# Layer 0's modulation columns beside attention: product on GpSimd, row sum on ScalarE, four transfer buffers

## The chip, the cores and the metric

One core of one Trainium2 chip. The metric is the device time of one execution in microseconds (us); of the kernel before three runs were timed.

## The reference

A batch of one sequence of 512 tokens of width 1024 goes through two blocks of two layers each. The first block is conditioned: its layers start from six modulation vectors, which are one matrix product with the activated condition.

```python
c_act = jax.nn.silu(c)
for l in range(DEPTH):
    mod = c_act @ w_mod[l] + b_mod[l]
    sh_m, sc_m, g_m, sh_f, sc_f, g_f = jnp.split(mod, 6, axis=-1)
    h = rms_norm(x, mix_norm_pre[l]) * (1.0 + sc_m[:, None, :]) + sh_m[:, None, :]
    y = hybrid_mixer(h, positions, w_in[l], ...)
    x = x + g_m[:, None, :] * rms_norm(y, mix_norm_post[l])
    h = rms_norm(x, ffn_norm_pre[l]) * (1.0 + sc_f[:, None, :]) + sh_f[:, None, :]
    y = swiglu(h, w_gate_up[l], w_down[l])
    x = x + g_f[:, None, :] * rms_norm(y, ffn_norm_post[l])
```

Here `c` is one row of 1024 numbers and `w_mod[l]` is 1024 x 6144. The hybrid mixer projects `h`, runs attention with 8 heads of 64 over keys chosen by an index score, runs an mLSTM with 4 heads of 128 beside it, and multiplies the joined heads with `w_out`. The second block has another mixer and no condition. Everything is float32.

## The kernel before, in words

**Modulation columns.** The kernel keeps features on the 128 partitions. The 6144 modulation numbers of a layer are 48 columns of 128. For each column the host has laid out its weights as a tile of 128x1024 (512 KB): row p holds the 1024 weights of feature p. With the activated condition spread over all partitions (`cc`, 128x1024), a column is the product of both tiles, summed along the row. The two layers of the first block have 96 such columns. Columns 0 to 15 (shift and scale of layer 0's mixer) are made before anything else; columns 16 to 39 (`MOD_FIRST` to `MOD_MIX`, 24 of them) beside layer 0's attention; the rest beside layer 0's feed-forward. The change touches the 24 only.

**The streamed weights.** All other weights pass through a ring of four slots of 128x1024. SP loads a slot (L160), ScalarE rounds it to `wh` (L171), GpSimd subtracts to get the rest `wl` (L182, in halves of 512 columns), and TensorE multiplies in three passes (L199 to L201). Each engine has one instruction queue that it takes in order; a wait at its head holds everything behind it.

**The first mixer** (`first_mixer`, used for layers 0 and 1) first runs 30 weight tiles (projections, index scores, the ranking of keys on VectorE, the mLSTM with its products L1022). Then follows attention, without weights from the ring: 32 items (4 blocks of 128 queries from the longest key range down, 8 heads), two in each step. It is written as a loop over steps p = 0 to 19 on each engine, with fixed lags:

- TensorE (L1058 scores of items 2p and 2p+1; L1069 turns the weights of step p-2; L1081 multiplies the weights of step p-3 with the values). In steps 3 to 6 it also turns one mLSTM head (L1090).
- VectorE: the masked row maximum of each score (L1412), one of two copies of turned weights from PSUM to SBUF (L1420, even items); in step 1 it scales the mLSTM results (L1450, four times), in steps 3 to 6 it gates one head (L1457, then L1461 after ScalarE's L1249), and at steps 7, 11, 15 and 19 it sums the squares of a finished block of queries (L1425).
- ScalarE: the copy for odd items (L1235), the exponentials with their row sums (L1227), the gate's rounding (L1249), and at steps 7, 11, 15 and 19 two readings of a finished block (L1244, L1245).

TensorE's turn of a step needs both copies of the step before; a copy needs the values of the same step to have released its buffer.

The 24 columns are spread over steps 2 to 19 on VectorE by `mods_at`, two in steps 4, 7, 10, 13, 16 and 19 and one in the others, at the end of a step (`modulate`, L1303: `tensor_tensor_reduce`, product and row sum in one instruction and a small read of the sum). SP's transfers for them (L877) stand behind its wait for the last mLSTM product (`mout`), and with two buffers, `mod_raw`, each waits for the product two before it:

```python
for n in range(MODS):
    if n == 0:
        sp.wait_ge(mout, MH)
    if n >= 2:
        sp.wait_ge(mod_used, n - 1)
    sp.dma_start(mod_raw[n % 2][:], a["wmod"][48 * rest_of + MOD_FIRST + n]).then_inc(mod_in[n % 2], 16)
```

SP goes on to the ring's loads for the out product after that. GpSimd has no work in attention: its next instruction is an L182 of the out product. The out product's first tiles were prepared before attention.

After step 19 VectorE waits for all 24 columns, adds the bias (L1469), finishes the squares (L1472, L1473); ScalarE, which has loaded the table for roots (L1265) by then, takes the root (L1267); VectorE inverts it (L1475) and scales the attention result (L1478, four times); TensorE turns it (L1110), and ScalarE (L1270) and VectorE (L1482) split it for the second half of the out product. TensorE takes the first half of the first two tiles of the out product, which needs only the mLSTM heads, before L1110.

Layer 1 runs the same code with `rest_of` at None: no columns, no `modulate`.

## Time and profile before

| what | us |
|---|---|
| median of 3 runs | 3232.46 |
| lowest and highest run | 3230.28, 3236.09 |
| the profiled execution's own time | 3230.66 |
| its span, first to last instruction | 3228.9 |
| TensorE busy in the span | 3098.0 (96%) |
| VectorE busy | 1626.8 (50%) |
| ScalarE busy | 1235.4 (38%) |
| GpSimd busy | 1367.8 (42%) |

The profile is of one execution. Its span is the time from the first to the last instruction; the own time has the start and end of the program around it. PE is TensorE's matmul, PEld its weight load, DVE is VectorE, ACT ScalarE, POOL GpSimd, SP SyncE with its DMA queue. Times in the timeline count from the span's start. Names of lines (L1303) are those of the kernel before. PEclk is TensorE's granted clock as a share of 2.4 GHz. "x24 | 29.3, 1224 | 12.3" reads: 24 instructions, 29.3 us busy, 1224 ns each in the mean, 12.3 us of idle time before them.

### The profile page before, as it was taken

Reading aid. Unit: us, or ns where it says so; the run is one execution under the profiler, and the core shown is the slowest. Engines: PE = TensorE matmul, PEld = TensorE weight load, DVE = VectorE, ACT = ScalarE, POOL = GpSimd, SP = SyncE. Lnnn points to the kernel's source line nnn. Section 1 sums busy time; section 2 is a strip of 40 time slices with the busy share of each in tenths; the row PEclk is TensorE's granted clock in tenths of the full one; section 3 lists DMA queues with packets and bytes.
Section 4 is the critical chain, followed back from the end, with each engine's and each line's share of the span. In section 5 each row is a group of like instructions: output and inputs, shape, how many; then the busy total and the mean of one; then the engine's idle time right before and its main releaser. Section 6 shows DMA issues by size and latency. Waiting matters only on the chain.

```text
span 3228.9 us, 39940 instructions
## 1 busy us (share of the span) xinstructions
PE 3098.0 (96%) x14974; PEld 2494.8 (77%) x14974; DVE 1626.8 (50%) x2738; ACT 1235.4 (38%) x2437; POOL 1367.8 (42%) x1167
## 2 busy tenths in 40 slices
PE   6998899999999999999999999999999999999998
PEld 5676778887766788887878788888887777788886
DVE  7787556623686553224344646554244345565521
ACT  3445332233345432232353534443325434343432
POOL 2340255544431254444432544444454234444443
PEclk9999799999999999999999999999999999999999
DMA  5422346622421132222321122222232111222222
GB/s 215 126 79 98 118 167 243 239 97 75 128 72 33 40 101 97 92 95 88 114 86 40 46 78 80 94 96 96 97 112 95 58 42 53 89 80 97 98 91 73
DMA packets 92976, 316.54 MB, mean 98 GB/s; under 512 B 12016, under 2 KB 12656, under 8 KB 92656
## 3 DMA queue, kind: packets, MB, share of 16 engines
q1 hardware_dynamic: 92784, 313.99, 29.1%
q8 instruction: 119, 1.95, 0.2%
q14 instruction: 73, 0.60, 0.1%
HBM read 301.36 MB, written 2.10 MB: 94 GB/s over the span
## 4 chain that ended last, share of the span: by engine, by line
PE 92%; DVE 4%; issue 2%; DMA 1%; ACT 1%; POOL 0%; SPq 0%; DVEq 0%; ACTq 0%; POOLq 0%
PE bank L199 24%; PE bank L201 24%; PE bank L200 24%; PE bank L1842 3%; PE bank L1800 2%; PE bank L1821 2%; PE bank L494 1%; PE bank L919 1%; PE bank L937 1%; PE bank L939 1%; PE bank L938 1%; PE bank L1081 1%; DMA mod_raw<-in_wmod 1%; PE bank L1905 1%; PE bank L1906 1%
## 5 line engine op out<-in xcount | busy, mean ns | idle before, releaser
L182 POOL TENSOR_TENSOR wl<-raw,wh 128x512 fp32r<-128x512 f32 (+1 forms) x952 | 1246.2, 1313 | 1692.8 <-ACT wh L171 1690.6
L171 ACT ACTIVATE wh<-raw 128x512 fp32r<-128x512 f32 (+1 forms) x952 | 587.3, 623 | 1437.3 <-PE bank L201 1340.5
L199 PE MATMUL bank<-hh,wh 128*128 128x512 f32 x2496 | 1005.7, 403 | 36.9 <-DVE hl L553 24.2
L201 PE MATMUL bank<-hh,wl 128*128 128x512 f32 x2496 | 983.5, 394 | 0.0
L200 PE MATMUL bank<-hl,wh 128*128 128x512 f32 x2496 | 983.3, 394 | 0.0
L199 PEld LDWEIGHTS bank<-hh,wh 128*128 128x128 f32 x2496 | 476.0, 191 | 164.0 <-DVE hl L553 30.6
L201 PEld LDWEIGHTS bank<-hh,wl 128*128 128x128 f32 x2496 | 475.3, 190 | 102.8
L200 PEld LDWEIGHTS bank<-hl,wh 128*128 128x128 f32 x2496 | 476.4, 191 | 95.7 <-issue 0.5
L201 PE MATMUL bank<-hidh,wl 128*128 128x512 f32 x704 | 280.8, 399 | 0.0
L200 PE MATMUL bank<-hidl,wh 128*128 128x512 f32 x704 | 277.4, 394 | 0.0
L199 PE MATMUL bank<-hidh,wh 128*128 128x512 f32 x704 | 276.0, 392 | 0.0
L381 DVE TENSOR_TENSOR bank<-x,y 128x512 f32<-128x512 f32 x49 | 63.1, 1289 | 318.7 <-ACT y L360 318.5
L200 PEld LDWEIGHTS bank<-hidl,wh 128*128 128x128 f32 x704 | 132.2, 188 | 34.4
L199 PEld LDWEIGHTS bank<-hidh,wh 128*128 128x128 f32 x704 | 132.2, 188 | 31.4
L201 PEld LDWEIGHTS bank<-hidh,wl 128*128 128x128 f32 x704 | 132.2, 188 | 30.5
L701 DVE SCALAR_TENSOR_TENSOR up<-bank,pc,up 128x511 f32<-128x511 f32 x88 | 65.9, 749 | 160.3 <-ACT up L681 158.8
L743 DVE CAST hidh<-hidden 128x512 fp32r<-128x512 f32 x88 | 123.2, 1400 | 3.0
L741 DVE TENSOR_TENSOR hidden<-gate,bank 128x512 f32<-128x512 f32 x44 | 30.0, 683 | 166.5 <-PE bank L201 158.1
L1968 ACT ACTIVATE tmp<-bank 128x128 f32<-128x128 f32 (+3 forms) x128 | 55.1, 438 | 138.6 <-PE bank L1842 137.1
L701 DVE SCALAR_TENSOR_TENSOR gate<-bank,pc,gate 128x511 f32<-128x511 f32 x88 | 65.9, 749 | 49.7 <-ACT gate L681 48.1
L2077 DVE CUSTOM_DVE_ANT_0 pr<-bank,cst 128x384 f32<-128x384 f32 (+3 forms) x84 | 38.2, 492 | 98.7 <-PE bank L1800 98.6
L490 POOL TENSOR_TENSOR x<-x,y 128x512 f32<-128x512 f32 x49 | 61.9, 1281 | 52.1 <-DVE y L541 52.1
(389 smaller groups left out, 3959.9 us busy)
## 6 DMA issues: line engine op xcount, KB each, us to landing
raw<-in_w SPq DMA_DIRECT2D x444, 512.0 KB, 3.4
mod_raw2a<-in_wmod SPq DMA_DIRECT2D x28, 512.0 KB, 4.5
mod_raw2b<-in_wmod SPq DMA_DIRECT2D x28, 512.0 KB, 5.0
mod_raw<-in_wmod SPq DMA_DIRECT2D x24, 512.0 KB, 3.6
raw<-in_w SPq DMA_DIRECT2D x32, 384.0 KB, 3.0
first_mods<-in_wmod SPq DMA_DIRECT2D x16, 512.0 KB, 13.8
tmp<-rawb SPq DMA_DIRECT2D x72, 64.0 KB, 2.4
turn<-sine SPq DMA_DIRECT2D x56, 64.0 KB, 2.0
```

The costliest lines, as they stand in the source:

```text
L171: act.activation(self.m.wh[:, t % 2, w_], self.m.raw[:, t % RING, w_], ACT.Copy)\
L182: pool.tensor_tensor(self.m.wl[:, t % 2, w_], self.m.raw[:, t % RING, w_], self.m.wh[:, t % 2, w_].bitcast(F32), ALU.subtract)\
L199: pe.matmul(out, wh, xh, start=start, stop=False)
L200: pe.matmul(out, wh, xl, start=False, stop=False)
L201: return pe.matmul(out, wl, xh, start=False, stop=stop)
L381: dve.tensor_tensor(dst, m.x[:, nb, :], m.y[:, nb, :], ALU.mult).then_inc(cross_ready, 1)
L490: pool.tensor_tensor(m.x[:, k, :], m.x[:, k, :], m.y[:, k, :], ALU.add).then_inc(x_ready, 1)
L701: return dve.scalar_tensor_tensor(buf[:, pair, shift:T], bank[:, 0:T - shift], m.pc[:, col:col + 1], buf[:, pair, shift:T], ALU.mult, ALU.add)
L743: step(dve.tensor_copy(hidh[:, q, :], hs[:, pair, :]))
L1800: pe.matmul(ps[one][:, 0:w_], q_, k_, start=True, stop=True).then_inc(score, 1)
L1821: ins = pe.transpose(ps[2 + one][:, kb * P:(kb + 1) * P], prs[i % 6][:, kb * P:(kb + 1) * P], ident)
L1842: ins = pe.matmul(bank[:, h * HD:(h + 1) * HD], m.tmp[:, one, kb * P:(kb + 1) * P], v_, start=(kb == 0), stop=(kb == tb))
```

## The change

The multiply moves to GpSimd: at the end of its work for the mixer's 30 tiles it runs through the 24 columns, waits for each transfer, and multiplies in place. ScalarE sums: at the end of each step, by the same `mods_at`, it waits for the product and runs a Copy over the 128x1024 tile with an accumulated row output into `m.mod`. VectorE no longer takes part; it still waits for `mod_used` after step 19. The two more buffers lie in the second half of `y`'s space, over the tail of `wt` and over `arg` of the mLSTM, which the last mLSTM product ends the use of. The transfer of column n now waits for the sum of column n - 4.

```diff
--- before.py
+++ after.py
@@ -785,7 +785,8 @@
     sc = [m.sq[:, 0, :], m.sq[:, 1, :], rawb[:, 0, :], rawb[:, 1, :]]
 
     cbc = Arena(nc, mix0 + 68 * 1024, D * 4)("cbc", [P, D])
-    mod_raw = [Arena(nc, vm_at + 4 * D * i, 4 * D)(f"mod_raw1{i}", [P, D]) for i in range(2)]
+    mod_raw = [Arena(nc, at, 4 * D)(f"mod_raw1{i}", [P, D])
+               for i, at in enumerate((vm_at, vm_at + 4 * D, y_at + 8 * D, y_at + 12 * D))]
     ang1 = Arena(nc, sel_at, T * 4)("ang1", [P, T])
     posi1 = nc.alloc_sbuf_tensor_at("posi1", [P, T], I32, offset=sel_at)
     turns1, rest1 = rawb[:, 0, :], rawb[:, 1, :]
@@ -797,7 +798,7 @@
     M1_SEMS = tuple(f"bank_free{b}" for b in range(8)) + (
         "latent_sq", "latent_sum", "latent_root", "latent_ready", "sine_ready", "swapped_in0", "swapped_in1", "swapped_in2", "rope_done",
         "conv_base", "conv_done", "ones_set", "order", "act_order",
-        "c_in", "c_act", "mod_in0", "mod_in1", "mod_used",
+        "c_in", "c_act", "mod_in0", "mod_in1", "mod_in2", "mod_in3", "mod_mult", "mod_used",
         "gate_log", "gate_sums", "m_exp", "wi_turned", "wi_ready", "rows_turned", "cols_ready",
         "iscore", "irelu", "irelu_used", "peak_row", "mscore", "arg_ready", "decay", "weight_ready", "masked",
         "mout", "mout_copied", "msums", "mroot_in", "mroot", "mscaled", "mturned", "gated_ready", "mhead",
@@ -812,13 +813,13 @@
         bank_free = sems[0:8]
         (latent_sq, latent_sum, latent_root, latent_ready, sine_ready, swapped_in0, swapped_in1, swapped_in2, rope_done,
          conv_base, conv_done, ones_set, order, act_order,
-         c_in, c_act, mod_in0, mod_in1, mod_used,
+         c_in, c_act, mod_in0, mod_in1, mod_in2, mod_in3, mod_mult, mod_used,
          gate_log, gate_sums, m_exp, wi_turned, wi_ready, rows_turned, cols_ready,
          iscore, irelu, irelu_used, peak_row, mscore, arg_ready, decay, weight_ready, masked,
          mout, mout_copied, msums, mroot_in, mroot, mscaled, mturned, gated_ready, mhead,
          early_ready, score, soft_in, weights, turned, copied_even, copied_odd, pv, out_copied,
          summed, root_in, root, ascaled, aturned, ahead, late_ready) = sems[8:]
-        mod_in, swapped_in = (mod_in0, mod_in1), (swapped_in0, swapped_in1, swapped_in2)
+        mod_in, swapped_in = (mod_in0, mod_in1, mod_in2, mod_in3), (swapped_in0, swapped_in1, swapped_in2)
         sines = rawb[:, 0, :], rawb[:, 1, :], qk[:, 6, :]
         turns_ = m.tmp[:, 0, :], m.tmp[:, 1, :], qk[:, 7, :]
 
@@ -872,9 +873,9 @@
             for n in range(MODS):
                 if n == 0:
                     sp.wait_ge(mout, MH)
-                if n >= 2:
-                    sp.wait_ge(mod_used, n - 1)
-                sp.dma_start(mod_raw[n % 2][:], a["wmod"][48 * rest_of + MOD_FIRST + n]).then_inc(mod_in[n % 2], 16)
+                if n >= 4:
+                    sp.wait_ge(mod_used, n - 3)
+                sp.dma_start(mod_raw[n % 4][:], a["wmod"][48 * rest_of + MOD_FIRST + n]).then_inc(mod_in[n % 4], 16)
 
         def gpsimd(pool):
             s.rests(pool, t0 + 2, t0 + 3)
@@ -888,6 +889,11 @@
                         pool.affine_select(out=w_, in_=w_, compare_op=ALU.is_ge, fill=0.0, base=0,
                                            pattern=[[1, P]], channel_multiplier=-1).then_inc(masked, 1)
                 s.rests(pool, t0 + t + 2, t0 + t + 3)
+            for n in range(MODS):
+                if n == 0:
+                    pool.wait_ge(c_act, 1)
+                pool.wait_ge(mod_in[n % 4], 16 * (n // 4 + 1))
+                pool.tensor_tensor(mod_raw[n % 4][:], mod_raw[n % 4][:], cc[:], ALU.mult).then_inc(mod_mult, 1)
 
         def tensor(pe):
             uses = [0] * 8
@@ -1249,6 +1255,12 @@
                 act.activation(m.hh[:, 4 + h, :], gated[:, h % 2, :], ACT.Identity,
                                scale=pa[:, A_MN + h:A_MN + h + 1]).then_inc(mhead, 1)
 
+            def collect(n):
+                at = 48 * rest_of + MOD_FIRST + n
+                act.wait_ge(mod_mult, n + 1)
+                act.activation(mod_raw[n % 4][:], mod_raw[n % 4][:], ACT.Copy,
+                               accum_out=m.mod[:, at:at + 1]).then_inc(mod_used, 1)
+
             for p in range(STEPS + 1):
                 if p >= VALUE_LAG + 4 and (p - VALUE_LAG) % 4 == 0:
                     finish((p - VALUE_LAG) // 4 - 1)
@@ -1262,6 +1274,8 @@
                     soften(2 * p + 1)
                 if MEND <= p < MEND + MH:
                     gate(p - MEND)
+                for n in mods_at.get(p, ()):
+                    collect(n)
             act.activation(idle4, m.eps[:, 0:1].to_broadcast([P, 4]), ACT.Sqrt)
             act.wait_ge(root_in, 1)
             act.activation(asum, asum, ACT.Sqrt, scale=1.0 / HD).then_inc(root, 1)
@@ -1294,14 +1308,6 @@
                 dve.wait_ge(swapped_in[r % 3], 64 * (r // 3 + 1))
                 dve.tensor_tensor(dst, dst, turns_[r % 3], ALU.add).then_inc(rope_done, 1)
                 dve.wait_ge(rope_done, r + 1)
-
-            def modulate(n):
-                if n == 0:
-                    dve.wait_ge(c_act, 1)
-                dve.wait_ge(mod_in[n % 2], 16 * (n // 2 + 1))
-                raw_, at = mod_raw[n % 2][:], 48 * rest_of + MOD_FIRST + n
-                dve.tensor_tensor_reduce(raw_, raw_, cc[:], 1.0, 0.0, ALU.mult, ALU.add,
-                                         m.mod[:, at:at + 1]).then_inc(mod_used, 1)
 
             freed = [1, 1, 1, 0, 1, 0, 0, 0]
             first_round = {t: sum(rounds_at.get(u, 0) for u in range(t)) for t in range(IN1 + 1)}
@@ -1461,8 +1467,6 @@
                     early(dve.scalar_tensor_tensor(m.hl[:, 4 + h, :], gated[:, h % 2, :],
                                                    pa[:, A_MN + h:A_MN + h + 1], m.hh[:, 4 + h, :].bitcast(F32),
                                                    ALU.mult, ALU.subtract))
-                for n in mods_at.get(p, ()):
-                    modulate(n)
             if MODS:
                 dve.wait_ge(mod_used, MODS)
                 rest = slice(48 * rest_of + MOD_FIRST, 48 * rest_of + MOD_MIX)
```

## Rows read from the trace of the kernel before

**Rows 1.** The page, part 1: busy time, share of the span, instructions.

```profile
PE 3098.0 (96%) x14974; PEld 2494.8 (77%) x14974; DVE 1626.8 (50%) x2738; ACT 1235.4 (38%) x2437; POOL 1367.8 (42%) x1167
```

**Rows 2.** Stretches: span, busy PE, PEld, DVE, ACT, POOL; clock; DMA share; GB/s.

```profile
276.95:353.43 76.48, 56.75 (x320) 48.28 (x320) 54.87 (x132) 30.35 (x83) 0.00 (x0) 0.75 0.50 165
1021.26:1073.83 52.57, 45.83 (x302) 38.88 (x303) 26.60 (x83) 28.77 (x82) 0.00 (x0) 0.86 0.00 1
```

**Rows 3.** The chain that ended last, 276.9 to 353.7, shares by line.

```profile
by line: DMA mod_raw<-in_wmod 29.7%; issue 14.4%; PE bank L1081 11.1%; PE bank L1069 10.0%; DVE mod_raw L1303 10.0%; DVE rawb L1412 4.7%; ACT pr L1227 3.7%; PE bank L1058 3.0%; DVE small L1425 2.3%; PE bank L1090 2.2%; DVE hl L1461 2.0%; AC
```

**Rows 4.** Groups of instructions of VectorE, 262 to 375.

```profile
L1303 DVE CUSTOM_DVE_ANT_0 mod_raw<-mod_raw,cc 128x1024 f32<-128x1024 f32 x24 | 29.3, 1224 | 12.3 <-DMA mod_raw<-in_wmod 11.7
```

**Rows 5.** The tile `mod_raw`, 266 to 269: its first two transfers.

```profile
L877 SPq DMA_DIRECT2D mod_raw<-in_wmod x2: 328/380/433, 267.1 to 267.5; - x2
...
DMA to landing us min/median/max: 3.6/4.1/4.5
```

**Rows 6.** Timeline of GpSimd up to 366; the bracket is idle time before.

```profile
365.10 1.30 POOL L182 TENSOR_TENSOR wl<-raw,wh 128x512 fp32r<-128x512 f32 x1 [101.42 <-ACT wh L171]
```

**Rows 7.** Groups of GpSimd's instructions by form, whole span.

```profile
L490 POOL TENSOR_TENSOR x<-x,y 128x512 f32<-128x512 f32 x49 | 61.9, 1281 | 52.1 <-DVE y L541 52.1
L182 POOL TENSOR_TENSOR wl<-raw,wh 128x256 fp32r<-128x256 f32 x32 | 23.6, 739 | 37.1 <-ACT wh L171 37.1
```

**Rows 8.** The line L182: duration min/median/max in ns.

```profile
L182 POOL TENSOR_TENSOR wl<-raw,wh x952: 738/1295/2357, 8.5 to 3201.4; 128x512 fp32r<-128x512 f32 x184, 128x256 fp32r<-128x256 f32 x7
```

**Rows 9.** Groups of ScalarE's instructions by form, whole span.

```profile
L1186 ACT ACTIVATE cc<-cc 128x1024 f32<-128x1024 f32 x1 | 1.1, 1062 | 0.0
```

**Rows 10.** Timeline of GpSimd at 1932.

```profile
1931.90 2.96 POOL L182 TENSOR_TENSOR wl<-raw,wh 128x512 fp32r<-128x512 f32 x2 [5.19 <-ACT wh L171]
```

**Rows 11.** Timeline of VectorE at 1932.

```profile
1931.99 1.75 DVE L2291 TENSOR_TENSOR y<-y,tmp 128x512 f32<-128x512 f32 x1
1933.77 1.64 DVE L2281 SCALAR_TENSOR_TENSOR hl<-y,hh 128x512 fp32r<-128x512 f32 x1
```

**Rows 12.** The line L541: duration min/median/max in ns.

```profile
L541 DVE TENSOR_TENSOR y<-y,bank x56: 671/676/689, 406.8 to 2850.9; 128x512 f32<-128x512 f32 x56
```

**Rows 13.** The lines L1450 and L1461, both layers.

```profile
L1450 DVE TENSOR_TENSOR num<-num,small x8: 691/692/693, 272.5 to 1019.0; 128x512 f32<-128x512 f32 x8
...
L1461 DVE SCALAR_TENSOR_TENSOR hl<-gated,pa,hh x8: 750/751/752, 284.6 to 1041.2; 128x512 fp32r<-128x512 f32 x8
```

**Rows 14.** ScalarE's waits, 1021.2 to 1041: us in total, times, longest.

```profile
ACT tmp L1235 <- PE bank L1081: 8.5, 4, 3.5
```

**Rows 15.** Timeline of TensorE in layer 0's attention.

```profile
296.52 3.51 PE L1081 MATMUL bank<-va,tmp 128*128 128x64 f32 x16
...
306.36 0.85 PE L1069 MATMUL bank<-cst,pr 128*128 128x128 f32 x6 [0.84 <-ACT pr L1227]
307.05 1.45 PE L1081 MATMUL bank<-va,tmp 128*128 128x64 f32 x12
```

**Rows 16.** Timeline of ScalarE in layer 0, then in layer 1.

```profile
302.32 0.58 ACT L1244 ACTIVATE att_n<-bank 128x512 f32<-128x512 f32 x1
...
353.65 0.23 ACT L1267 ACTIVATE small<-small 128x32 f32<-128x32 f32 x1 [8.17 <-DVE small L1473]
...
1040.98 0.58 ACT L1244 ACTIVATE att_n<-bank 128x512 f32<-128x512 f32 x1
...
1045.07 0.19 ACT L1227 ACTIVATION_READ_ACCUMULATOR pr<-rawb,small 128x1 f32 x1
...
1072.86 1.28 ACT L1265 ACT_TABLE_LOAD   x1
...
1074.27 0.21 ACT L1267 ACTIVATE small<-small 128x32 f32<-128x32 f32 x1
```

**Rows 17.** Stretches of layer 0, columns as in rows 2.

```profile
295.00:303.00 8.00, 8.00 (x37) 6.75 (x35) 5.05 (x11) 3.99 (x11) 0.00 (x0) 0.50 0.36 112
...
322.00:346.00 24.00, 17.89 (x78) 15.70 (x77) 15.40 (x42) 9.27 (x30) 0.00 (x0) 0.52 0.61 196
```


## The prediction

> **What bounds the kernel now.** The page comes first: TensorE is 96% busy [rows 1], so only stretches in which it waits or runs thin can be won. The stage in question is layer 0's attention, and the trace holds a measure for it: layer 1 runs the same code without modulation columns. Set side by side [rows 2], from the same point (TensorE's turn of step 3, after an equal wait, 276.95 and 1021.26) to the same small instruction (L1473, which starts at 353.43 and 1073.83), layer 0 takes 76.5 us and layer 1 52.6. The columns cost 23.9 us today. That is the ceiling of any gain, 0.74% of the span. VectorE is busy 54.9 us in the first stretch and 26.6 in the second, ScalarE about 30 in both.
>
> The chain of waits says how the 23.9 come about: 29.7% of it lies on the landing of a column, 10.0% on VectorE's product [rows 3]. There are 24 products of 1.22 us, and VectorE stands idle 11.7 us for their transfers [rows 4]: with two buffers, a transfer of 3.6 us or more [rows 5] starts only when a product has ended. GpSimd does nothing for 101.42 us up to 365.10 [rows 6].
>
> **The change, part by part.** It takes the 24 products and the 11.7 us of waits out of VectorE's order, has GpSimd multiply and ScalarE sum, and adds two buffers. The transfers stay on SP's queue behind the same first wait; the ring's weight loads queue behind them as before, and the out product starts from ring slots filled earlier, so this costs nothing while the last column is issued no later than now, as it is in the working below.
>
> *GpSimd's product, M.* No GpSimd instruction over 1,024 columns is in the trace. L182 takes 0.739 us for 256 [rows 7] and 1.295 for 512 [rows 8]: 256 columns add 0.556, so 1,024 take 1.295 + 2 x 0.556 = 2.41, an estimate. I take 2.4. Bounds: 2.3, and 2.9 (L182 reaches 2.36 at 512, 1.06 over its median; half of that on each product). 24 products are 57.6 us on an idle engine: room enough in 76 us, not in 52.
>
> *ScalarE's sum.* The Silu over 128x1024 took 1.06 us [rows 9], and the read of a row sum takes 0.19 (L1227 in [rows 16]), part of which I take to lie under the next instruction. I take 1.15, bounds 1.06 and 1.25. 24 are 27.6 us on ScalarE, what VectorE loses. ScalarE waits for GpSimd before each sum, and behind it in its order stand the copies of turned weights that TensorE waits for.
>
> *The shared port.* This is the term against the change. At 1931.9 GpSimd ran two L182 back to back in 2.96 us instead of 2.6 [rows 10]; beside them VectorE's L2291 and L2281, with two SBUF operands each, took 1.75 and 1.64 us [rows 11] instead of the 0.69 of such an instruction alone. They took turns: the second VectorE instruction did not follow the first but waited 0.95, one GpSimd instruction less 0.35. A VectorE instruction with one operand in PSUM does not stretch (L541, 56 times, 0.671 to 0.689) [rows 12]. So the maxima and copies of attention, which read PSUM, are free of it. Two places aren't: L1450, four times in a row from 272.5, and L1461, once in each of steps 3 to 6 [rows 13]. No row shows either beside a busy GpSimd.
> L1450: the first column lands at 267.1 + 3.6 = 270.7 [rows 5]; GpSimd holds the port to about 272.8, and three more columns have landed behind it. The first L1450 (wanted at 272.5) waits 0.3, the next three one product each, 2.4 - 0.35 = 2.05: 0.3 + 6.15 = **6.5 us**, all on the path, since step 2's maximum and the copy that TensorE's turn needs stand behind it. Bounds 0.3 (VectorE keeps the port once it has it) and 8 (M at its bound).
> L1461: GpSimd is busy about half of that time, so four times half of 2.05 = **4.1**, bounds 0 and 8.2.
> The Trainium skill (SBUF — State Buffer, "Who interferes with whom") says that a VectorE instruction with two SBUF inputs and a GpSimd instruction that reads SBUF exclude each other, and that the second is blocked until the first has finished. By whole instructions each of the three waits would be 2.4, 1.05 us more in the sum; the row gives 0.35 less, and the row is used.
>
> *Steps 2 to 6 otherwise.* ScalarE's six sums there fall mostly into its waits for TensorE before a copy (8.5 us in four places of layer 1) [rows 14]: 0.5. TensorE stands idle some 10 us from 273 and comes back at the lower of its two granted clocks (1.2 GHz), where 16 matmuls of values take 3.51 us; 12 at the upper take 1.45, so 16 take 1.93 [rows 15]. One such step partly: 1.0.
>
> So ScalarE begins the first block's end (L1244) at layer 1's 1040.98, which is 296.7 in layer 0's time (744.3 less), plus 6.5 + 4.1 + 0.5 + 1.0 = **308.8**; before it was 302.3 [rows 16]. At this point the new kernel is 6.5 us late.
>
> *From there GpSimd and the ring of buffers set the pace.* The sum of column 6 ends 4.3 (L1244 to the end of the second exponential's read, 1040.98 to 1045.26 [rows 16]) and 1.15 later, at 314.25. Its buffer takes column 10: 0.1 to issue, 3.6 to land, 317.95. Columns 10 to 23 are 14 products, 33.6 us. One gap lies between: column 16 needs the sum of 12, which on ScalarE ends 15.4 after that of 6, while the six products take 14.4: 1.0. (The 15.4: step 7's second sum 1.15; steps 8 and 9 a copy of 0.4 and then TensorE's turn and values, 0.85 + 1.45 [rows 15] + 0.2 of signals = 2.5 each; step 10 a copy 0.35, two exponentials and two sums 3.3, the next block's end 1.15; step 11 a copy 0.3, the exponentials behind VectorE's row sum 2.2, a sum 1.15.) GpSimd ends at 352.55. ScalarE alone would be done some 3.7 earlier: its own work is hidden behind GpSimd's by that much and no more. Last sum 1.2: 353.75.
> The tail: before, ScalarE loaded the root's table (L1265) in idle time; now the load stands behind the last sum. Layer 1, where it is exposed, has 1.41 from its start to L1267: with 0.1 of signal L1267 comes at 355.25, against 353.65 before [rows 16]. What follows is the same code. **Sum: 1.6 us later.** The transfer waits and VectorE's share are won; the port, the slower multiplier and the table load give it back.
>
> The profiled execution's own time is 3230.66 (the span 3228.9 and 1.8 around it), 1.8 under the median of the runs, 3232.46. I put the 1.6 on the median: 3234.1, told as 3234. A measurement of this kernel can tell about 0.2%, 6.5 us, from no change.
>
> **The rivals.**
> *A, the port costs nearly nothing*: VectorE's four L1450 go through in one piece, and L1461 meets gaps. For: VectorE asks again at once. Against: in [rows 10, 11] GpSimd's waiting instruction came first just there. Then L1244 starts at 298.2, sum 6 ends at 303.65, column 10 starts at 307.35, GpSimd ends at 341.95 and L1267 comes at 344.65, 9.0 earlier than now: **3223.5**. Faster, 0.2.
> *B, TensorE's clock*, the case on the slower side. Behind each of ScalarE's copies lie TensorE's turn and values; my 2.5 us are at the upper clock. The granted clock was 0.50 from 295 to 303 and 0.52 from 322 to 346 [rows 17]. At that, 2.5 become 4.6: steps 8 and 9 add 2.1 each, step 10 adds 0.8 and steps 12 to 14 add 1.3, all of which widens the gaps before columns 16 and 17, since there ScalarE has no cover. 6.3 + 1.6 = 7.9, **3240.4**. It decides once nearly all these steps fall into the low clock; against it, the turn and values at 306 ran at the upper one [rows 15]. 0.2.
> *C, GpSimd's product is longer.* Each 0.1 us of M costs 14 + 3 + 2 (the last for L1461) = 19 times that. From M = 2.66 on it is a loss beyond 0.2%; at 2.9 it is 9.5 + 1.6: **3243.6**. For: L182's maximum [rows 8]. Against: L490, at 1.281 in 49 instances [rows 7], is below L182. 0.08.
> *D, the change doesn't do what it says*: GpSimd could be held by weight work ahead of the products in its order. Its idle time before 365.10 began at 263.7 [rows 6], ahead of the first column. 0.02, no difference.
>
> **How the numbers follow.** My forecast, no change, has 0.5; its own range is 3229 to 3239 (L1461 from 0 to 8.2, a sum from 1.06 to 1.25). A gives faster 0.2; B and C give slower, 0.28; the 0.02 of D and of the forecast's edges go to both sides: 0.20, 0.50, 0.30. The range reaches from A less 1.5 to the end of C: 3222 to 3244.
>
> **What would show it.** Right: L1450 four times some 2.8 us apart, in turns with GpSimd; GpSimd's 128x1024 near 2.4; L1461 at up to 2.8; ScalarE's sums waiting for GpSimd in steps 16 to 19, and GpSimd without idle time from about 333; the table load behind the last sum; VectorE without a wait on a transfer. Wrong: L1450 at 0.69 and the block's end before 300 (A); the low clock from 308 to 330 (B); products over 2.6 (C). It would also be wrong if ScalarE and not GpSimd were the engine without idle time at the end.

## The result, and the profile after

| | before | after |
|---|---|---|
| median of 20 runs each (us) | 3233.28 | 3238.49 |
| lowest and highest run | 3226.81, 3241.71 | 3231.25, 3243.18 |
| ratio, with its 95% interval | | 1.0015, 1.0008 to 1.0021 |
| span of the profiled execution | 3228.9 | 3240.6 |

The change costs about 0.15%, some 4.8 us by the ratio (the two medians lie 5.2 apart): below the 0.2% that was called telling, on the slower side, and with an interval that leaves out a gain. The two profiled spans differ by 11.7, but the stage of the change holds only half of that; the rest lies in code that the change doesn't touch (last section). The execution of after that was profiled took 3242.28, 3.8 over its median.

The page of after, part 1, answers to [rows 1]. VectorE's share falls, ScalarE's and GpSimd's rise, and TensorE stays at 96%:

```profile
PE 3112.7 (96%) x14974; PEld 2507.3 (77%) x14974; DVE 1611.8 (50%) x2690; ACT 1258.2 (39%) x2485; POOL 1422.2 (44%) x1191
```

Lines of after stand 6 to 14 below those of before here: L1450 is L1456, L1461 is L1467, L1244 is L1250, L1267 is L1281, L1081 is L1087. The product is L896, the sum L1261.

**The start of attention.** The timelines of VectorE and of GpSimd in after (start, us, line, how many, idle time before):

```profile
272.08 9.45 DVE L1456 TENSOR_TENSOR num<-num,small 128x512 f32<-128x512 f32 x4
```

```profile
270.37 10.61 POOL L896 TENSOR_TENSOR mod_raw<-mod_raw,cc 128x1024 f32<-128x1024 f32 x4 [7.10 <-DMA mod_raw<-in_wmod]
```

The four scalings, 2.87 us before (four of 0.69, [rows 13]), take 9.45, with the longest at 2.725, and cover the same time as GpSimd's first four products: the two engines take turns. TensorE stands behind them. Its timeline answers to [rows 15]; the turn of step 3 waited 3.87 before:

```profile
283.14 1.94 PE L1075 MATMUL bank<-cst,pr 128*128 128x128 f32 x8 [10.46 <-ACT pr L1233]
...
285.72 3.52 PE L1087 MATMUL bank<-va,tmp 128*128 128x64 f32 x16
```

**The columns.** The tile `mod_raw` in after, answering to [rows 4, 5]:

```profile
L896 POOL TENSOR_TENSOR mod_raw<-mod_raw,cc x24: 2343/2368/2917, 270.4 to 354.1; 128x1024 f32<-128x1024 f32 x24
L1261 ACT ACTIVATE mod_raw<-mod_raw x24: 1040/1044/1062, 284.4 to 356.6; 128x1024 f32<-128x1024 f32 x24
...
  DMA mod_raw<-in_wmod: 34.7, 12
```

VectorE's wait for columns (11.7) is gone; GpSimd now waits for them, 34.7 us, though there are four buffers. Its timeline from step 7 on says when:

```profile
317.28 6.98 POOL L896 TENSOR_TENSOR mod_raw<-mod_raw,cc 128x1024 f32<-128x1024 f32 x3 [3.53 <-DMA mod_raw<-in_wmod]
325.55 2.37 POOL L896 TENSOR_TENSOR mod_raw<-mod_raw,cc 128x1024 f32<-128x1024 f32 x1 [1.29 <-DMA mod_raw<-in_wmod]
329.95 4.67 POOL L896 TENSOR_TENSOR mod_raw<-mod_raw,cc 128x1024 f32<-128x1024 f32 x2 [2.03 <-DMA mod_raw<-in_wmod]
335.81 2.35 POOL L896 TENSOR_TENSOR mod_raw<-mod_raw,cc 128x1024 f32<-128x1024 f32 x1 [1.19 <-DMA mod_raw<-in_wmod]
338.74 2.36 POOL L896 TENSOR_TENSOR mod_raw<-mod_raw,cc 128x1024 f32<-128x1024 f32 x1 [0.58 <-DMA mod_raw<-in_wmod]
342.26 6.99 POOL L896 TENSOR_TENSOR mod_raw<-mod_raw,cc 128x1024 f32<-128x1024 f32 x3 [1.16 <-DMA mod_raw<-in_wmod]
349.45 7.11 POOL L896 TENSOR_TENSOR mod_raw<-mod_raw,cc 128x1024 f32<-128x1024 f32 x3 [0.20 <-DMA mod_raw<-in_wmod]
```

From column 10's product at 317.28 there are 14 products and six gaps, 6.45 us together. Each gap is a transfer that started late, because the sum that frees its buffer came late in ScalarE's order. What ScalarE's order follows is seen on TensorE, in the same stretch:

```profile
315.31 1.54 PE L1075 MATMUL bank<-cst,pr 128*128 128x128 f32 x6
316.64 2.66 PE L1087 MATMUL bank<-va,tmp 128*128 128x64 f32 x12
319.23 1.23 PE L1064 MATMUL bank<-kT,qT 64*128 64x256 f32 x4
320.39 1.11 PE L1075 MATMUL bank<-cst,pr 128*128 128x128 f32 x4
321.30 2.66 PE L1087 MATMUL bank<-va,tmp 128*128 128x64 f32 x12
323.89 1.23 PE L1064 MATMUL bank<-kT,qT 64*128 64x256 f32 x4
325.04 1.11 PE L1075 MATMUL bank<-cst,pr 128*128 128x128 f32 x4
```

No idle time stands here: TensorE itself is the bound, at its lower clock, with 12 matmuls of values in 2.66 where they took 1.45 before [rows 15]. The chain that ended last, 283 to 358, says the same of this part and says what ends the stage. The four lines of TensorE hold 45.6% of it; its last pieces are one transfer and three products of GpSimd in a row:

```profile
by line: PE bank L1087 23.9%; PE bank L1075 12.4%; ACT mod_raw L1261 10.9%; POOL mod_raw L896 9.5%; issue 8.0%; ACT pr L1233 7.9%; PE bank L1064 6.2%; DMA mod_raw<-in_wmod 4.6%; PE bank L1096 3.1%; DVE rawb L1418 2.9%; ACT acc L1251 2.4%; A
...
345.91 3.47 DMA mod_raw<-in_wmod
349.45 7.12 POOL mod_raw L896 x3
```

Stretches of before and after side by side (columns as in [rows 2]: span, busy PE, PEld, DVE, ACT, POOL; granted clock; DMA share; GB/s). Before:

```profile
310.00:320.00 10.00, 7.16 (x58) 6.09 (x58) 7.70 (x22) 5.16 (x17) 0.00 (x0) 1.00 0.68 215
320.00:330.00 10.00, 8.43 (x41) 7.77 (x41) 8.17 (x25) 3.50 (x14) 0.00 (x0) 0.56 0.56 185
```

After:

```profile
310.00:320.00 10.00, 9.00 (x44) 7.88 (x44) 3.99 (x15) 6.60 (x17) 6.07 (x4) 0.59 0.50 170
320.00:330.00 10.00, 8.49 (x40) 6.92 (x36) 2.46 (x9) 6.93 (x19) 6.68 (x4) 0.50 0.43 130
330.00:340.00 10.00, 9.67 (x46) 8.67 (x46) 3.18 (x18) 7.70 (x24) 8.23 (x4) 0.50 0.46 151
```

**The end.** ScalarE's timeline, answering to [rows 16]: the last sum, the table load behind it, the root, at 359.17 where it was 353.65.

```profile
356.59 1.06 ACT L1261 ACTIVATE mod_raw<-mod_raw 128x1024 f32<-128x1024 f32 x1 [1.21 <-POOL mod_raw L896]
...
357.76 1.28 ACT L1279 ACT_TABLE_LOAD   x1
...
359.17 0.21 ACT L1281 ACTIVATE small<-small 128x32 f32<-128x32 f32 x1
```

### The profile page after: what moved, and what is told of

It is laid out like the page before. It is cut to its first block, busy times and chain, and to the rows that moved or that the text cites. A ratio compares the mean times of both kernels' runs of the same rounds, so it can differ in the third digit from the quotient of the medians.

```text
span 3240.6 us, 39954 instructions
## 1 busy us (share of the span) xinstructions
PE 3112.7 (96%) x14974; PEld 2507.3 (77%) x14974; DVE 1611.8 (50%) x2690; ACT 1258.2 (39%) x2485; POOL 1422.2 (44%) x1191
## 3 DMA queue, kind: packets, MB, share of 16 engines
q8 instruction: 119, 1.95, 0.2%
## 4 chain that ended last, share of the span: by engine, by line
PE 88%; DVE 7%; ACT 2%; issue 2%; DMA 1%; POOL 0%; SPq 0%; DVEq 0%; ACTq 0%; POOLq 0%
PE bank L199 23%; PE bank L201 23%; PE bank L200 23%; PE bank L1846 3%; PE bank L1804 2%; PE bank L1825 2%; PE bank L1087 1%; DVE sel L1320 1%; DVE small L1319 1%; PE bank L494 1%; PE bank L925 1%; DVE qk L1376 1%; PE bank L1909 1%; PE bank L1910 1%; PE bank L1908 1%
## 5 line engine op out<-in xcount | busy, mean ns | idle before, releaser
L182 POOL TENSOR_TENSOR wl<-raw,wh 128x512 fp32r<-128x512 f32 (+1 forms) x952 | 1242.3, 1309 | 1610.7 <-ACT wh L171 1608.5
L490 POOL TENSOR_TENSOR x<-x,y 128x512 f32<-128x512 f32 x49 | 61.9, 1278 | 54.3 <-DVE y L541 54.3
```

The costliest lines, as they stand in the source:

```text
L182: pool.tensor_tensor(self.m.wl[:, t % 2, w_], self.m.raw[:, t % RING, w_], self.m.wh[:, t % 2, w_].bitcast(F32), ALU.subtract)\
L490: pool.tensor_tensor(m.x[:, k, :], m.x[:, k, :], m.y[:, k, :], ALU.add).then_inc(x_ready, 1)
```

## The experiments

**The measure** of all of them is one stretch: from TensorE's first scores of attention to ScalarE's root. Before it is 353.65 - 267.01 = 86.6; after 359.17 - 266.61 = 92.6, so +5.9, of the size of the +4.8 of the runs; layer 1, without columns, 1074.27 - 1011.32 = 62.95. The start is where attention becomes possible in all of them (266.4 to 267.5). The theory after the result: the shared port takes 6.6 at the start; then the pace of columns, set by GpSimd's product and ScalarE's sum together with TensorE's lower clock, takes the rest and eats what the buffers bring.

| kernel | first scores to root (us) | ratio to before, 95% | same stretch in layer 1 (us) |
|---|---|---|---|
| before | 86.6 | | 63.0 |
| after | 92.6 | 1.0015 (1.0008 to 1.0021) | 71.7 |
| e1, GpSimd starts behind the scalings | 84.2 | 0.9990 (0.9979 to 1.0002) | 65.4 |
| e2, four buffers on VectorE, nothing moved | 77.8 | 0.9968 (0.9957 to 0.9980) | 72.6 |
| e3, short sum | 89.3 | 1.0001 (0.9989 to 1.0012) | 65.4 |
| e4, short product | 82.0 | 0.9971 (0.9960 to 0.9981) | 67.5 |
| e5, every second column moved | 81.7 | 0.9994 (0.9984 to 1.0003) | 72.6 |
| e6, e1 with six buffers | 83.5 | 0.9979 (0.9967 to 0.9990) | 72.7 |
| e7, table load earlier | 92.2 | one run, 3242.86 us | 72.7 |
| e8, TensorE kept busy in step 3 | 92.9 | 1.0009 (0.9998 to 1.0021) | 63.3 |
| e9, e1 with short sum and product | 70.7 | 0.9957 (0.9942 to 0.9971) | 61.9 |
| e10, every third column moved, six buffers | 81.6 | 0.9987 (0.9975 to 0.9999) | 70.2 |

The times are from one profiled execution each. The last column says how far such a time can be trusted: layer 1's attention is the same code in all twelve kernels, and it took 61.9 to 72.7 us. The stretch in before and in after (columns as in [rows 2]):

```profile
1011.32:1074.27 62.95, 52.30 (x328) 41.80 (x328) 34.76 (x103) 38.20 (x107) 0.00 (x0) 0.87 0.00 1
```

```profile
1017.56:1089.22 71.66, 63.88 (x328) 51.58 (x328) 34.79 (x103) 37.95 (x107) 0.00 (x0) 0.70 0.00 1
```

VectorE and ScalarE do the same work in the same time; the granted clock is 0.87 and 0.70, and TensorE is busy 11.6 us longer. So a difference between two rows of the table is safe only where the ratios bear it out, with intervals that don't meet: e1, e2 and e4 against after, e9 against e1, e5 against e2. They don't part e3 or e8 from after, e6 from e1, or e10 from e2, and those of e1 and e2 touch.

### e1: the port at the start

```diff
                 if n == 0:
                     pool.wait_ge(c_act, 1)
+                    pool.wait_ge(mscaled, NT)
```

> The changed kernel, but GpSimd's first product waits until VectorE's four scalings of step 1 (L1456 of the changed kernel, L1450 before) have ended; the transfers start as before. Measure: attention from TensorE's first scores to ScalarE's root, 86.6 us before, 92.5 us changed. Theory (the shared port): the four scalings go from 9.45 back to 2.9 us, and the measure falls by 6 to 7, to about 86. Rival 1 (the four transfers that land at 268 to 274 disturb VectorE): the scalings stay at 9.4, measure 92.5. Rival 2 (GpSimd's pace sets the end, so its later start eats what VectorE wins): scalings 2.9, measure still 91 to 93.

Measured: 84.2, 8.4 less than after. The scalings in VectorE's timeline and GpSimd's first products:

```profile
272.99 2.87 DVE L1457 TENSOR_TENSOR num<-num,small 128x512 f32<-128x512 f32 x4
```

```profile
275.99 11.63 POOL L897 TENSOR_TENSOR mod_raw<-mod_raw,cc 128x1024 f32<-128x1024 f32 x5 [11.80 <-DVE num L1457]
```

GpSimd starts 4.7 us later, counted from the first scores (275.99 against 270.37), and the stage ends earlier. So the early start was worth less than it cost: the 6.6 on the scalings lay on the path. The other 1.8 of the 8.4 is not explained by them. The port has not gone, either: L1461 (L1468 in e1), 0.75 alone, now meets GpSimd each time and takes 1.79, 2.15, 1.95 and 2.17, which is 5.1 in all.

With this one wait the moved columns are level with before or a little under.

### e2: the buffers alone

The kernel before with `mod_raw` in four places, as in the diff of the change, `n % 4`, and SP's wait at `n - 3`; product and sum stay on VectorE.

> The kernel before with four transfer buffers and nothing else: product and sum stay on VectorE. Theory (VectorE's 11.7 us of waits for transfers were the larger half of what the columns cost): no waits for a column, measure 86.6 less 8 to 11 = 76 to 79, device time 8 to 10 us under before. Rival (VectorE's products, not the transfers, set the steps, and waits only move to TensorE): measure 84 to 87, no difference.

Measured: 77.8, 8.8 less than before, and the lowest ratio of any kernel that computes everything, 0.9968. The tile `mod_raw` there:

```profile
L1304 DVE CUSTOM_DVE_ANT_0 mod_raw<-mod_raw,cc x24: 1214/1224/1226, 277.9 to 343.2; 128x1024 f32<-128x1024 f32 x24
...
  DMA mod_raw<-in_wmod: 1.2, 1
```

The wait of 11.7 falls to 1.2. Against this the moving of the work, the rest of the change, costs 92.6 - 77.8 = 14.8.

### e3 and e4: which engine's work counts

```diff
-                act.activation(mod_raw[n % 4][:], mod_raw[n % 4][:], ACT.Copy,
+                act.activation(mod_raw[n % 4][:, 0:8], mod_raw[n % 4][:, 0:8], ACT.Copy,
```

> The changed kernel, but ScalarE's sum takes only 8 of the 1024 products of each column (this leaves out the sum of the other 1016). Theory (ScalarE's 24 sums of 1.04 us delay its copies and hold the buffers, and that makes GpSimd idle): measure 92.5 less 12 to 16 = 76 to 80, GpSimd's idle time from the 10th column on near 0. Rival (GpSimd's 24 products of 2.37 us set the pace by themselves): measure 89 to 92.

Measured: 89.3. The theory that ScalarE's share of the work holds the steps fell; 24 sums cut from 1.04 to 0.19, some 20 us of work less, bring 3.3, which is the 89 to 92 of the rival. The windows say why:

```profile
320.00:330.00 10.00, 9.85 (x44) 7.94 (x44) 3.25 (x13) 5.61 (x22) 5.31 (x3) 0.50 0.40 139
330.00:340.00 10.00, 10.00 (x50) 8.97 (x48) 2.39 (x15) 4.79 (x28) 9.34 (x4) 0.50 0.55 190
```

TensorE is busy all the time, at the lower clock, with ScalarE half idle. Time given to ScalarE is not taken up while TensorE is the bound. From 330 on GpSimd is busy as well (9.34 of 10 us), and the end is its own: six products in a row from 340.64 to 354.64, behind a transfer of 3.54.

e4 multiplies a quarter of each column:

```diff
-                pool.tensor_tensor(mod_raw[n % 4][:], mod_raw[n % 4][:], cc[:], ALU.mult).then_inc(mod_mult, 1)
+                pool.tensor_tensor(mod_raw[n % 4][:, 0:256], mod_raw[n % 4][:, 0:256], cc[:, 0:256], ALU.mult).then_inc(mod_mult, 1)
```

> The changed kernel, but GpSimd multiplies only 256 of the 1024 columns (this leaves out three quarters of the product). Theory: the four scalings of step 1 take about 2.9 + 4 x 0.4 = 4 to 5 us instead of 9.45, which gives 5, and near the end nobody waits for GpSimd, which gives 3 more; the sums of ScalarE stay: measure 84 to 86. Rival (GpSimd's pace sets the end everywhere): measure 76 to 80. Rival (the port is not the cause of the long scalings): scalings still 9.4.

Measured: 82.0, 10.6 less than after, a little more than expected. The scalings took 3.71 instead of 9.45, which is 5.7 of it. At the end, after has 13.3 from the start of the last transfer on its chain to the root (345.91 to 359.17), e4 has 9.1 (339.28 to 348.34): three products of 2.37 have become one of 0.73, while the transfer takes 5.65 instead of 3.47. That is another 4.2. The middle, again at a clock of 0.50 from 310 to 340, gives next to nothing (0.7).

### e5: every second column moved

`modulate` is back on VectorE for even columns; GpSimd and ScalarE take the odd ones, from the scalings' end on; four buffers.

```diff
-                    sp.wait_ge(mod_used, n - 3)
+                    sp.wait_ge((mod_used, mod_summed)[n % 2], (n - 4) // 2 + 1)
...
-            for n in range(MODS):
+            for n in range(1, MODS, 2):
```

> Columns in turn on two paths: even ones on VectorE (product and sum in one, as before), odd ones on GpSimd and ScalarE (as changed), four buffers, GpSimd's first product behind the four scalings. Measure: TensorE's first scores of attention to ScalarE's root; 86.6 us before, 92.6 changed, 84.2 with GpSimd's late start, 77.8 with four buffers alone, 63.0 in layer 1 without columns. Theory (each step carries a column's work on one engine's order, and halving it on each lets it fall into waits): 70 to 75, device time 12 to 15 us under before. Rival (TensorE at its lower clock sets the steps, whoever multiplies): 76 to 79, no better than four buffers alone.

Measured: 81.7, worse than either expectation and 3.9 over e2, which moves nothing. The tile's lines:

```profile
L897 POOL TENSOR_TENSOR mod_raw<-mod_raw,cc x12: 2350/2364/3344, 275.0 to 343.2; 128x1024 f32<-128x1024 f32 x12
L1319 DVE CUSTOM_DVE_ANT_0 mod_raw<-mod_raw,cc x12: 1215/1328/3154, 277.0 to 343.7; 128x1024 f32<-128x1024 f32 x12
...
  POOL mod_raw L897: 6.6, 2
```

VectorE's own column product, 1.22 in e2, goes up to 3.15 when it meets GpSimd's, and ScalarE waited 6.6 for GpSimd near the end. There the last transfer took 6.63 (from 336.52) and stood on the chain that ended last, with GpSimd's product behind it.

### e6: more buffers

e1 with `mod_raw` in six places (`y_at + 4 * D` and the start of the mLSTM's rows besides), `n % 6` and SP's wait at `n - 5`.

> The changed kernel with six buffers instead of four, and GpSimd's first product behind the four scalings. In the run with four buffers and this start GpSimd stood idle 16.4 us for transfers. Theory (GpSimd's 24 products and its waits for buffers set the end): idle time of GpSimd 3 to 8 us, measure 84.2 less 8 to 12 = 72 to 76. Rival (ScalarE's order of copies, exponentials and 27.6 us of sums sets the end): measure 81 to 84, GpSimd's waits for transfers turn into ends earlier than ScalarE's.

Measured: 83.5, only 0.7 under e1; the expectation of 72 to 76 fell, and the rival's 81 to 84 came. GpSimd still waited 14.4 for transfers, but ScalarE never waited for GpSimd. The windows:

```profile
310.00:320.00 10.00, 10.00 (x45) 8.26 (x44) 2.53 (x10) 5.28 (x17) 7.00 (x3) 0.50 0.45 156
...
340.00:350.00 10.00, 9.59 (x30) 7.52 (x30) 1.84 (x6) 9.94 (x21) 6.45 (x3) 0.55 0.46 158
```

First TensorE is busy without a break (310 to 320), in the end ScalarE (9.94 of 10 us): the steps pay for TensorE at its lower clock, and the last steps, where the sums stand thickest, pay for ScalarE. On the chain that ended last, 320 to 351, ScalarE's sums hold 37.3% and no product of GpSimd stands. Neither asks for a buffer.

### e7: the table load

```diff
             for p in range(STEPS + 1):
...
+                if p == STEPS:
+                    act.activation(idle4, m.eps[:, 0:1].to_broadcast([P, 4]), ACT.Sqrt)
                 for n in mods_at.get(p, ()):
                     collect(n)
-            act.activation(idle4, m.eps[:, 0:1].to_broadcast([P, 4]), ACT.Sqrt)
```

> The changed kernel, but ScalarE loads the root's table before the sums of step 19 instead of behind them. The sums are a Copy, and the theory takes it that they run with the root's table as well: from the end of the last sum to the root 0.5 to 0.9 us instead of 1.4, measure 92.6 less 0.5 to 0.9. Rival: the Copy needs another table, and a second load appears behind the sums: 1.4 or more as before.

Measured: 92.2. ScalarE's timeline at the end:

```profile
354.17 1.28 ACT L1278 ACT_TABLE_LOAD   x1
...
358.88 0.23 ACT L1282 ACTIVATE small<-small 128x32 f32<-128x32 f32 x1 [0.70 <-DVE small L1478]
```

Two sums run behind the load and no second load follows, so the sum may stand on either side of it. The root is 0.7 behind the last sum instead of 1.41, now waiting for VectorE's L1478: half of the 1.41 was only the load's. But GpSimd's last product is late in any case, and the stretch shows just 0.4, which a single execution can't tell from nothing. The Trainium skill (ScalarE: Activation LUTs, "Table sets: the hidden batching unit") says that cheap functions such as copy come with every table set; by that rule the sums need no load of their own, and the trace agrees.

### e8: the clock in steps 3 to 6

Fourteen matmuls of scores that nobody reads, into a free bank, in TensorE's wait of 10.46 us (the trace has two entries for each, 28):

```diff
+                if MODS and p == 3:
+                    for _ in range(14):
+                        pe.matmul(ps[7][:], qT[0:64, 0, 3 * P:4 * P], kT[0:64, 0, :], start=True, stop=True)
```

> The changed kernel, and TensorE runs 14 more score matmuls into an unused bank (their result is overwritten) behind the scores of step 3, in the 10.5 us in which it waits for the four scalings. Theory (the wait brings TensorE down to the lower clock, and steps 3 and 4 pay for it): the turn of step 3 takes 1.1 us instead of 1.94 and the values of step 3 1.9 instead of 3.52; measure 92.6 less 3 to 4 = 88 to 90. Rival (the matmuls run late into the step and cost what the clock gives): 92 to 94.

Measured: 92.9. The timeline of TensorE:

```profile
272.42 12.18 PE L1105 MATMUL bank<-kT,qT 64*128 64x512 f32 x28
284.52 1.09 PE L1075 MATMUL bank<-cst,pr 128*128 128x128 f32 x8
...
285.89 1.90 PE L1087 MATMUL bank<-va,tmp 128*128 128x64 f32 x16
```

With TensorE busy, the upper clock is kept (granted 1.00 from 267 to 290, against 0.73 in after): the turn takes 1.09 instead of 1.94 and the values 1.90 instead of 3.52. The filling overran the wait by 1.4 (284.52 against 283.14), and the block's end on ScalarE came at 307.06, 0.7 earlier than in after. Yet from 310 to 320 the granted clock is 0.50 again, and the end is not earlier.

So the lower clock right behind the long wait cost about 2 us (0.7 at the block's end and the 1.4 that the filling itself took), and the lower clock from 310 on came without it. The length of the wait does not decide alone: before, e1 and e2 all have a wait of 3.87 in this place, and behind it the same 16 matmuls took 2.20, 3.52 and 3.51.

### e9: both short

e1 with the cuts of e3 and e4 together.

> After, with GpSimd starting only when the four scalings are done, GpSimd multiplying 256 of a column's 1024 and ScalarE summing 8 of them; the transfers stay whole. The other 768 products and 1016 terms of each sum are left out, so its time is that of transfers, waits and instructions alone. Measure: from TensorE's first scores to ScalarE's root (before 86.6, after 92.6; late start alone 84.2, short sum alone 89.3, short product alone 82.0; layer 1 without columns 62.95). Theory 1, either engine's work alone is enough to hold the steps, and the low clock is only what follows from TensorE waiting for them: with both short 64 to 68, so 16 to 20 us under the late start alone, and the granted clock over 0.80 in 310 to 350. Theory 2, TensorE's low clock carries on by itself from step 7 on, whatever the two engines do: 78 to 81, clock under 0.60. A third, the transfers set the pace once both are short: GpSimd idle on transfers over 35 us and 70 to 76.

Measured: 70.7, 13.4 under e1. Theory 2 falls: the lower clock does not carry on whatever the two engines do. Theory 1 falls too, by its time and by the clock of 0.62 from 330 to 340. The windows:

```profile
310.00:320.00 10.00, 7.80 (x65) 6.58 (x64) 4.81 (x19) 6.44 (x27) 2.19 (x3) 0.99 0.58 194
320.00:330.00 10.00, 7.20 (x50) 6.22 (x48) 3.52 (x18) 6.84 (x35) 2.91 (x4) 0.86 0.80 263
330.00:340.00 10.00, 9.23 (x30) 7.22 (x29) 3.07 (x8) 4.25 (x16) 3.65 (x5) 0.62 0.71 263
```

The time is that of the third theory, 70 to 76, and GpSimd's wait for transfers is 42.8. That wait alone shows little (it was 33.0 in e3), but the chain that ended last does: two transfers, 7.00 us from 323.32 and 4.02 from 331.48, make up 11 of the 13.3 us from there to the table load. So with both engines' work cut short the transfers end the stage.

### e10: every third column moved, six buffers

The six places are those of e6. VectorE takes 16 columns, GpSimd and ScalarE 8; each waits only for its own column six before.

```diff
+                    if n % 3 == 2:
+                        sp.wait_ge(mod_summed, (n - 6) // 3 + 1)
+                    else:
+                        sp.wait_ge(mod_used, (n - 6) - (n - 6) // 3 + 1)
```

> Six buffers; VectorE multiplies and sums 16 of the 24 columns as in the kernel before, every third goes by GpSimd (from the scalings' end on) and ScalarE; each path waits only for its own column six before. Nothing is left out. Measure: first scores to root (four buffers on VectorE alone 77.8, every second column by the other path and four buffers 81.7, late start alone 84.2). Theory 1, the split by two failed for want of buffers: with six the 14.9 us that 24 columns on VectorE cost over layer 1 shrink by a third to 9.9, 72.9, and the shared port gives back 1 to 4: 74 to 77, wait for transfers under 3 on VectorE. Theory 2, the port and ScalarE's part cost what VectorE's share saves: each of eight GpSimd products of 2.4 us holds VectorE's product beside it by up to 2.0, and eight sums stand in ScalarE's order: 78 to 82.

Measured: 81.6, theory 2. Six buffers and fewer moved columns did not make the split pay, though they took the waits away: ScalarE waited for GpSimd once, 1.0, VectorE for a transfer never. VectorE's and GpSimd's timelines show the port between two column products:

```profile
305.78 3.41 DVE L1323 CUSTOM_DVE_ANT_0 mod_raw<-mod_raw,cc 128x1024 f32<-128x1024 f32 x1
...
327.96 2.68 DVE L1323 CUSTOM_DVE_ANT_0 mod_raw<-mod_raw,cc 128x1024 f32<-128x1024 f32 x1
```

```profile
305.75 2.36 POOL L901 TENSOR_TENSOR mod_raw<-mod_raw,cc 128x1024 f32<-128x1024 f32 x1 [9.32 <-DMA mod_raw<-in_wmod]
...
327.20 2.35 POOL L901 TENSOR_TENSOR mod_raw<-mod_raw,cc 128x1024 f32<-128x1024 f32 x1 [6.89 <-DMA mod_raw<-in_wmod]
```

GpSimd started 0.03 earlier and VectorE's product took 1.22 + 2.19; with GpSimd 0.76 ahead, 1.22 + 1.46. In both, VectorE finished about 1.05 after GpSimd's end: it ended 1.08 and 1.09 after GpSimd's did, so it waits for GpSimd's instruction up to the last 0.15 us or so, and then does its own. The clock was 0.50 from 310 to 340 here too. The two waits put 3.7 us back into VectorE's order, of the 8 x 1.22 = 9.8 that leave it, and eight sums put 8 x 1.04 = 8.3 into ScalarE's. By how much each of the two makes e10 slower than e2 was not measured apart; the intervals of their ratios overlap.

## Why the prediction was right, and where not

The forecast, no change that 0.2% can show, held: 3234 predicted, 3238.5 measured, +4.8 by the ratio where +1.6 was worked out. In the profiled stage it is +5.5 at the root (359.17 against 353.65). By the steps of the sum:

- **The port at L1450, 6.5**: measured 9.45 - 2.87 = 6.58, on the path, and e1 takes it away. The taking of turns that [rows 10, 11] showed once between other instructions holds here. Rival A falls with it. The Trainium skill (SBUF — State Buffer, "Who interferes with whom") lets the second engine wait for the whole instruction of the first. With products of 2.37 that gives 0.3 + 3 x 2.37 = 7.4; the trace has 6.58, so nearer to the row's 0.35 less.
- **M, 2.4**: measured median 2.368, once 2.917. Rival C falls.
- **ScalarE's sum, 1.15**: a pair of sums back to back is 1.04 apart (311.98 and 313.02); the read lies wholly under what follows. 0.1 too much each.
- **The port at L1461, 4.1**: mis-sized. Four took 4.2 in sum instead of 3.0: 1.2. I had GpSimd busy half of that time; between 281 and 303 it was busy for two products, 4.7 of 22 us, since all four buffers held products that waited for their sums, and ScalarE's first sum came only at 284.4. In e1, where the products start later, the same four take 8.1, 5.1 over: the meetings go where GpSimd's work goes.
- **Steps 2 to 6 otherwise, 1.5**: mis-sized the other way. ScalarE's L1250 came at 307.79 with the first scores 0.4 earlier, so 307.79 + 0.4 - 296.7 = 11.5 late in all; less 6.6 and 1.2 that leaves 3.7. Some 2 of it is the lower clock, which e8 lifts: it held for two steps, values 3.52 and 2.55 against 1.9. The rest was not taken apart. The two misses nearly cancel, which is why 308.8 was forecast and 308.2 came (307.79, counted from the first scores of before): by luck a right subtotal out of two wrong terms.
- **The tail, 1.4**: table load to root 1.41, as forecast.
- **GpSimd sets the pace from column 10, with one gap of 1.0**: this is the step that failed. The product began as forecast (317.28 against 317.95), and 14 products took 0.8 less than 33.6, but six gaps took 6.45, so GpSimd ended at 356.56 instead of 352.55. That is all of the miss. The term behind it that was mis-sized is TensorE's turn and values in steps 8 and 9, put at 2.5 us from the end of a copy to the next one, at the upper clock. ScalarE's L1241 starts at 314.32, 319.40 and 324.05, with 0.49 for each copy, so the two took 4.6 and 4.2, at a clock of 0.59 and then 0.50, and ScalarE, forecast 3.7 ahead of GpSimd, freed the buffers too late. From turn to turn TensorE took 5.1 and 4.7 (315.31, 320.39, 325.04) without a pause. The same two steps of before took 3.7 and 2.5 (310.25 to 313.91 to 316.39), the second also without a pause, but at the upper clock. So in these steps TensorE, not GpSimd, set the pace.

The rows of before for the second of the two steps:

```profile
313.91 0.63 PE L1069 MATMUL bank<-cst,pr 128*128 128x128 f32 x4 [0.90 <-ACT pr L1227]
...
316.39 0.66 PE L1069 MATMUL bank<-cst,pr 128*128 128x128 f32 x4
```

The failed step is rival B's mechanism, in the steps that rival B named: it had 6.3 more for the gaps, and they grew by 5.45. I had argued against it with one row at 306 that ran at the upper clock. That the time still lies nearer to the forecast than to rival B's +7.9 comes from two terms that came out lower, 0.7 up to column 10 and 0.8 for the products. So the forecast held in part by luck. That the low clock causes the gaps is read from this one execution; no run lifts the clock there and leaves the rest.

The ceiling of 23.9 us was not a ceiling, either. It sets layer 0 against layer 1 of one execution, and layer 1's 62.95 there is near the lowest of the twelve traces; in e2's execution layer 0 took 77.8 and layer 1, without any column, 72.6. The start of the sum, 296.7 for L1244, is taken from the same layer 1 and shares its clock.

What I had not seen is how little the moved work would be worth even without the port. The 23.9 us were read as a sum of waits and VectorE's work. e2 shows the waits for transfers to be worth 8.8 of it. Moving the work to engines that looked idle, with the same buffers and the port's worst case taken out (e1), is 6.4 worse than leaving it where it was (84.2 against 77.8; by the ratios 7). The port is in that still, up to 5.1 at the four L1461. e5, e6 and e10 end between 81.6 and 83.5, each by another way. By the stretch the sum alone is worth 3.3 and the product 10.6, of which 5.7 is the port at the scalings; together, with the port away, they are worth 13.4, more than the parts. The ratios say otherwise: 4.5 for the sum, 14.2 for the product, 8.1 for the late start and 10.7 for both behind it, so the parts just add up (4.5 + 14.2 - 8.1 = 10.6). Whether one engine's saving goes into the other's waits is therefore not shown, though in the traces of e3 and e4 the clock from 310 to 340 was 0.50 and TensorE busy for most of it.

What stays open is why the granted clock falls where it does. From 300 to 310 and from 310 to 320 it was 1.00 and 0.59 in after, 0.80 and 1.00 in before, 0.50 and 0.98 in e2, 0.84 and 0.82 in e1, 0.56 and 0.50 in e6, 0.67 and 0.99 in e9. TensorE's waits do not settle it as far as these traces go: layer 1, the same code in all of them, ran at 0.87 in before and at 0.68 in e2. No run changes TensorE's waits alone at that place; e8 did so at 275 only. Layer 1 shows that up to 10.8 us between two traces can be due to this and not to an edit. Only one execution of after was traced, so whether the others have the low clock in the same steps is not known.

## What to carry to other kernels

Split a change into its parts before judging it: here four buffers alone win 0.32% and the move of engines gives all of it back. An idle GpSimd is not free help for VectorE where VectorE reads two SBUF operands; count each such meeting as up to one GpSimd instruction of waiting, and look first at what stands at the moment when GpSimd's first inputs arrive. And price the steps behind a moved instruction at both of TensorE's clocks when the rows show both, since a stage that is made of waits can turn into one that TensorE bounds. Before a stage's time in one trace is taken for the effect of an edit, or another layer's time for a ceiling, look at how much a stage of the same code differs between traces: here 10.8 us.

## What the runs showed of the hardware that was not expected

- VectorE behind GpSimd at the shared port waits in a chain: four VectorE instructions of 0.69 us met four GpSimd ones of 2.37, and the row of four took 9.45 instead of 2.87, the longest 2.725, as if each of the later three had let one of GpSimd's pass first, although no other VectorE work stood between them. In e5 and e10 a single VectorE product went from 1.22 to as much as 3.41.
- In a single meeting the engine that started second paid. In e5 VectorE's product began at 306.72, 0.12 ahead of GpSimd's, and took its 1.23; GpSimd's took 3.33 instead of 2.36. In e10 GpSimd's began 0.03 ahead and took its 2.36; VectorE's took 3.41 instead of 1.22. GpSimd lost about 1 us at most, VectorE up to 2.2.
- A Copy with an accumulated row output ran behind the load of the root's table without another load (e7).
- Work that nobody reads holds TensorE's upper clock through a wait (e8, 1.09 and 1.90 against 1.94 and 3.52), but was worth 0.7 us at the next mark and nothing at the end.
- Two profiled executions can differ by more than a change is worth: of the 11.7 us between the spans of before and after 5.9 lie in the stage, while layer 1's attention, whose code is untouched, took 8.7 more at a granted clock of 0.70 instead of 0.87. Over the twelve traces this stretch took 61.9 to 72.7 us. The 20 runs of the kernel before lie up to 8.4 us from their median.
